# A fused two-block kernel: TensorE products of the identity placed in front of its waits

## The chip, the cores and the metric

The kernel runs on one core of one Trainium2 chip, as one launch. The time is the device time of the whole program in microseconds, taken as the median of several runs. One further run was recorded by the hardware profiler; every row below comes from it.

## The reference

The program computes a first transformer block and then a second block of two layers, for 256 tokens of width 1024 in float32.

- First block: a modulation vector from `c`; `h = modulate(rms_norm(x))`; a token mixer with a retention branch (4 heads) and three groups of dilated attention (12 heads), merged by gates and multiplied by `w_o`; `x = x + g1 * mixer`; then an MLP, `x = x + g2 * (relu(h @ w_ff1)**2) @ w_ff2` with 4096 hidden columns; a final RMS norm.
- Each of the two layers of the second block: an input projection of x; multi-head latent attention (8 heads), an mLSTM (4 heads, two directions) and an SSD scan (4 heads, two directions), whose outputs are joined and multiplied by `w_out`; a residual and a layer norm; then a two-level mixture of experts: router products pick one of 4 groups and 2 of its 4 experts per token, tokens are sorted by group, 16 experts of width 256 are applied, and the result is scattered back; a residual and a layer norm.

## The kernel before, in words

The five engines run programs of their own, written out in order by hand, and meet in semaphores. Weights stream from HBM in units of 128x1024 into a ring of 8 raw slots (SyncE issues the DMAs). ScalarE rounds a unit to `w_hi` (L679), GpSimd or VectorE subtracts to get `w_lo` (L622, L1945), into rings of 4 slots, and TensorE multiplies each unit in three products (`mm3`: hi by hi, hi by lo, lo by hi, L1162 to L1164). A slot is handed on when TensorE increments `unit_used`.

Activations reach TensorE as transposed halves. `turn_x` (L1211) transposes four 128x128 tiles of x or h for each of two halves into the two banks of `T`, and for each half waits for `ready` (VectorE has written it) and for the bank of `T` to be read; ScalarE copies the result (`xT_hi`), VectorE subtracts (`xT_lo`, L1951) and increments `t_lo`. `up_normed` starts a stage: `turn_x` for token tile 0, products of that tile with units 0 to 2, `turn_x` for token tile 1, products with unit 3, then the second tile's products with units 0 to 3. It starts the mixer of the first block, the MLP and each layer.

In the first block's MLP, `clear_acc` zeroes the four banks of `AC`, and `ffn_step` then waits for the squared ReLU (`ffn_h`), transposes it (`turn`, L1288) and runs the products of the next hidden tile.

In a layer, a loop over p (0 to 14, with `N_POS2` = 12) runs at each position some products of the projection and some pieces of the attention: `mla_scores`, `mla_turn` (L1622), `mla_values` (L1632, which waits for ScalarE's copy and VectorE's release). The mixers' loop over h (0 to 4, `LH` = 4) has rows, products and then `ssd_values` (L1745, waits for GpSimd, L658) and `lstm_values` (L1737). After the output product comes the router: `turn_x` for token tile 0, four of its eight router chunks, `turn_x` for tile 1, the other chunks (L1805 to L1808, products with 40 and 20 columns). The routing then waits for VectorE twice: for the chosen group before the ranks (L1823 to L1828), and for the one-hot slots before `gather` (L1835). The experts follow.

PSUM has 8 banks: `T` two, `G` two, `AC` four. TensorE's order is fixed: what stands behind a wait waits too.

Of the kernel before, what the change touches and what calls it, by code (L numbers as in the profile page):

```python
# [25 lines left out]
P = 128  # L26
S = 256
TOK = S // P
# [16 lines left out]
LH, LDH = 4, 64  # L45
# [28 lines left out]
U_MLP = U_WO + 8  # L74
# [4 lines left out]
N_ADA = len(ADA_ORDER)  # L79
# [6 lines left out]
L_IN = 0  # L86
# [4 lines left out]
N_POS2 = 3 * UP  # L91
# [26 lines left out]
LT_X = 0  # L118
# [74 lines left out]
def program(nc, A):  # L193

    ctx = ExitStack()
    with ctx:
# [962 lines left out]
        def _(pe):  # L1159
# [41 lines left out]
                if t == TOK - 1:  # L1201
                    i.then_inc(unit_used, 1)

            def turn_x(n, t, src, ready, at):

                for b in range(2):
                    pe.wait_ge(ready, at + b + 1)
                    if not (isinstance(n, int) and n + b < 2):
                        pe.wait_ge(t_lo, n + b - 1)
                    for c in range(4):  # L1210
                        i = pe.transpose(T[:, b, c * P:(c + 1) * P], src[:, t, b * NT + c * P:b * NT + (c + 1) * P], ident[:, :])  # L1211
                    i.then_inc(t_ready, 1)

            def up_normed(n, k, banks, tn, src, ready, at, turned=None):


                def half(t, u):

                    if u % (UP // HALVES) == 0:
                        pe.wait_ge(t_lo, tn + 2 * t + u // (UP // HALVES) + 1)  # L1220

                turn_x(tn, 0, src, ready, at)
                if turned:
                    turned()
                for u in range(UP):
                    if u == UP - 1:
                        turn_x(tn + 2, 1, src, ready, at + HALVES)
                    half(0, u)
                    up_tile(n, k, u, 0, banks)
                for u in range(UP):  # L1230
                    half(1, u)
                    up_tile(n, k, u, 1, banks)
# [79 lines left out]
            def clear_acc():  # L1312
                for b in range(4):
                    pe.matmul(AC[:, b, :], zero_r[0:1, :], xT_hi[0:1, 0:2, :].rearrange("p c n -> p (c n)"),
                              start=True, stop=False)
# [200 lines left out]
            down_pairs(0, U_WO, T_MERGE, lambda q: tile(10 + q // 2)[:, :, q % 2 * 256:(q % 2 + 1) * 256], 4, merged_head)  # L1516

            mod_sums(5)
            up_normed(0, U_MLP, G, T_H2, h_sb, h_ready, HALVES * TOK, lambda: pe.wait_ge(mod_out, N_ADA))
            pe.wait_ge(zero_ready, 1)  # L1520
            clear_acc()
            with pe.Fori(0, FF_TILES - 2) as e:
                ffn_step(e * 8 + U_MLP, UP, e * 2 + T_MLP, e, tile(1), 4)
            e = FF_TILES - 2
# [15 lines left out]
            for l in range(LAYERS):  # L1540
                n = l * L_UNITS + U_LAYERS
                tb = l * LT + T_LAYERS
                m = l * LM + (M_LAYERS + G_CREDIT)
                up_normed(n, L_IN, G, tb + LT_X, x_sb, x_ready, HALVES * l * TOK)
                for u in range(UP):
                    if u == UP - 1:
                        pe.wait_ge(cq_ready, l + 1)
# [88 lines left out]
                def mlstm_rows(h):  # L1636

                    for j in (2 * h, 2 * h + 1):
                        if j >= 2:
                            pe.wait_ge(lexp_ready, l * 8 + (j - 1))  # L1640
                        row(AC[:, j % 2, :], j % 2 * LH + h, (mask_f, mask_b)[j % 2]).then_inc(lrow_ready, 1)
# [31 lines left out]
                for p in range(N_POS2 + 3):  # L1673
                    if p == 0:
                        pe.wait_ge(kv_out, l * TOK + TOK)
                    if p == UP:
                        pe.wait_ge(q_out, l + 1)
                    if p == 2 * UP:
                        pe.wait_ge(g_free, m + 3)
                    if p < N_POS2 - 2:  # L1680
                        up_unit(n, L_REST + p // UP * UP, p % UP, (G, AC, G)[p // UP])
                    elif p < N_POS2 + 2:
                        half = p - (N_POS2 - 2)
                        up_tile(n, L_REST + N_POS2 - UP, UP - 2 + half // TOK, half % TOK, G)
                    if p in (1, 2):
                        mla_qk_turn(2 * p - 2)
                        mla_qk_turn(2 * p - 1)
                    if p == 3:
                        for k in range(4, 8):
                            mla_qk_turn(k)  # L1690
                    if p == 4:
                        pe.wait_ge(q_out, l + 1)
                        running_sums()
                        conv_turn(0)
                        conv_turn(1)
                    if p == 5:
                        conv_turn(2)
                        pe.wait_ge(sx_out, l * 3 + 2)
                        pe.wait_ge(rows_w, l + 1)
                        for t in range(TOK):  # L1700
                            i = pe.transpose(T[:, 1, t * P:(t + 1) * P], rows_p[:, t, :], ident[:, :])
                        i.then_inc(rows_T, 1)
                    if 4 <= p < 4 + MH:
                        mla_scores(p - 4)
                    if 6 <= p < 6 + MH:
                        if p == 6:
                            pe.wait_ge(sx_out, l * 3 + 3)
                            pe.wait_ge(rows_out, l + 1)
                        mla_turn(p - 6)
                    if p == N_POS2 + 2:  # L1710
                        pe.wait_ge(row_ready, l + 1)
                        pe.wait_ge(lqk_out, l * TOK + TOK)
                        mlstm_rows(0)
                    if 7 <= p < 7 + MH:
                        mla_values(p - 7)
                    if p == N_POS2 + 2:
                        ssd_inputs()
                    if p == 8:
                        pe.wait_ge(g_free, m + 4)
                        for t in range(TOK):  # L1720
                            for c in range(4):
                                a = IN2["mq"] + c * P
                                i = pe.transpose(AC[:, t, c * P:(c + 1) * P], P2[:, t, a:a + P], ident[:, :])
                            i.then_inc(lqk_T, 1)
# [41 lines left out]
                for h in range(LH + 1):  # L1766
                    if h < LH:
                        if h == 0:
                            pe.wait_ge(me_ready, l * MH + MH)
                        for j in (2 * h, 2 * h + 1):  # L1770
                            if j >= 2:
                                pe.wait_ge(sexp_ready, l * 8 + (j - 1))
                            elif j == 1:
                                pe.wait_ge(scb_out, l * SG + 1)
                            row((AC[:, 2, :], T[:, 1, :])[j % 2], 8 + j % 2 * SH + h, (mask_f, mask_b)[j % 2]).then_inc(srow_ready, 1)
                        if h == 0:
                            lstm_products(0)
                        if h + 1 < LH:
                            lstm_products(h + 1)
                            mlstm_rows(h + 1)  # L1780
                    if h >= 1:
                        ssd_values(h - 1)
                        lstm_values(h - 1)
# [7 lines left out]
                nr = EGROUPS + EXPERTS  # L1791

                turn_x(tb + LT_X2, 0, x_sb, x2_ready, HALVES * l * TOK)
                pe.wait_ge(lo_ready, n + (L_ROUTER + 1))
                s = L_ROUTER % SLOTS

# [2 lines left out]
                def router(t, chunks):  # L1799

                    both = AC[:, t, 0:2 * nr].rearrange("p (x n) -> p x n", x=2)
                    for c in chunks:
                        rows = slice(t * P, (t + 1) * P)
                        if c < KC - 1:
                            pe.matmul(both, xT_hi[:, c, rows], w_both[:, :, c, :], start=c == 0, stop=False)  # L1805
                        pe.matmul(both[:, 0, :], xT_lo[:, c, rows], w_both[:, 0, c, :], start=False, stop=False)
                        if c == KC - 1:
                            i = pe.matmul(both, xT_hi[:, c, rows], w_both[:, :, c, :], start=False, stop=True)  # L1808
                            return i

                pe.wait_ge(t_lo, tb + (LT_X2 + 1))
                router(0, range(KC // 2))
                pe.wait_ge(t_lo, tb + (LT_X2 + 2))
                turn_x(tb + (LT_X2 + 2), 1, x_sb, x2_ready, HALVES * (l * TOK + 1))
                router(0, range(KC // 2, KC))
# [2 lines left out]
                pe.wait_ge(t_lo, tb + (LT_X2 + 4))  # L1818
                router(1, range(KC // 2, KC)).then_inc(unit_used, 1)

                pe.wait_ge(route_in, l * 4 + 1)
                rank = AC[:, 2, 0:12].rearrange("p (k n) -> p k n", n=4)
                pe.matmul(rank[:, 2, :], ones, r_g[:, 0, :], start=True, stop=False)  # L1823
# [6 lines left out]
                def gather(q):  # L1830
# [5 lines left out]
                                              start=t == 0 and x is xk_hi, stop=t == 1 and x is xk_lo)  # L1836
                    i.then_inc(t_ready, 1)

                pe.wait_ge(route_in, l * 4 + 3)
                for q in range(UP):  # L1840
                    gather(q)
# [1159 lines left out]
```

## Time and profile before

| | us |
|---|---|
| median of 3 runs | 1404.49 |
| lowest, highest | 1401.08, 1404.7 |
| profiled run, its own time | 1406.39 |
| profiled run, span of the core | 1404.3 |
| TensorE busy (share of the span) | 1309.3 (93%) |
| VectorE busy | 857.3 (61%) |
| ScalarE busy | 735.1 (52%) |
| GpSimd busy | 635.4 (45%) |

The span runs from the first to the last instruction on the core. Times in rows are microseconds from the span's start. TensorE's clock is granted by the chip at one of two levels; a stretch's figure is the mean share of 2.4 GHz, so 0.50 is 1.2 GHz throughout, and a figure between 0.50 and 1.00 is part of each.

### The profile page before, as it was taken

What the parts mean: (1) busy time and instruction counts of PE and PEld (TensorE: products, weight loads), DVE (VectorE), ACT (ScalarE), POOL (GpSimd) and SP (SyncE); (2) the same over time, 40 slices, a digit from 0 to 9 for tenths busy, and PEclk for the clock granted to TensorE, in tenths of its full rate; (3) what the DMA queues carried; (4) which work ended last, traced back from release to release, by engine and by line L of the source; (5) the groups of instructions that cost most, each with busy time, mean ns of one, the idle gap of its engine ahead of it and who ended that gap; (6) DMA issues with size and microseconds to landing.
All of it is one profiled execution on the core that took longest, in us unless ns stands there. A gap on an engine that the chain in (4) does not pass through costs nothing.

```text
span 1404.3 us, 17484 instructions
## 1 busy us (share of the span) xinstructions
PE 1309.3 (93%) x6096; PEld 1066.3 (76%) x6096; DVE 857.3 (61%) x1349; ACT 735.1 (52%) x1090; POOL 635.4 (45%) x516
## 2 busy tenths in 40 slices
PE   6899999999998899999998979999989997799996
PEld 3687777888886688887787767888868786788884
DVE  7574873354344543113677667877867857677778
ACT  4343444454564444445566416666745653467664
POOL 2899889987768689997400410000060024000000
PEclk9999999999999999999999879999999989799998
DMA  9966468635444455454531007878744300577782
GB/s 380 365 237 239 152 237 307 240 150 240 181 154 160 163 180 183 176 200 159 210 121 61 0 15 304 306 291 327 289 190 151 120 1 0 222 294 282 287 308 90
DMA packets 44477, 279.86 MB, mean 199 GB/s; under 512 B 5453, under 2 KB 8781, under 8 KB 12014
## 3 DMA queue, kind: packets, MB, share of 16 engines
q1 hardware_dynamic: 37426, 263.82, 50.6%
q10 hardware_dynamic: 6974, 15.05, 2.9%
q8 instruction: 44, 0.72, 0.2%
q14 instruction: 33, 0.27, 0.1%
HBM read 274.66 MB, written 4.19 MB: 199 GB/s over the span
## 4 chain that ended last, share of the span: by engine, by line
PE 74%; DVE 10%; POOL 8%; DVEq 3%; ACT 2%; issue 2%; DMA 1%; ACTq 0%; SPq 0%; POOLq 0%
PE G L1162 12%; PE G L1164 11%; PE G L1163 11%; PE AC L1162 9%; PE AC L1164 9%; PE AC L1163 9%; POOL w_lo L622 8%; DMA w_raw<-w_stream 1%; DVE w_lo L1945 1%; PE T L1288 1%; DVE arena L2542 1%; ACT w_hi L679 1%; PE G L1737 1%; PE G L1745 1%; DVE sm L1981 1%
## 5 line engine op out<-in xcount | busy, mean ns | idle before, releaser
L622 POOL TENSOR_TENSOR w_lo<-w_raw,w_hi 128x512 fp32r<-128x512 f32 (+1 forms) x474 | 607.3, 1314 | 360.6 <-ACT w_hi L679 352.7
L679 ACT ACTIVATE w_hi<-w_raw 128x1024 fp32r<-128x1024 f32 x448 | 470.8, 1056 | 404.6 <-PE G L1164 192.4
L1945 DVE TENSOR_TENSOR w_lo<-w_raw,w_hi 128x1024 fp32r<-128x1024 f32 x230 | 278.4, 1223 | 65.0 <-ACT w_hi L679 57.3
L1162 PE MATMUL AC<-w_hi,yT_hi 128*128 128x512 f32 x464 | 183.6, 396 | 0.9 <-POOL w_lo L622 0.9
L1162 PE MATMUL G<-w_hi,xT_hi 128*128 128x512 f32 x432 | 178.3, 413 | 3.7 <-DVE xT_lo L1951 1.9
L1163 PE MATMUL AC<-w_lo,yT_hi 128*128 128x512 f32 x464 | 180.9, 390 | 0.0
L1164 PE MATMUL AC<-w_hi,yT_lo 128*128 128x512 f32 x464 | 180.8, 390 | 0.0
L1164 PE MATMUL G<-w_hi,xT_lo 128*128 128x512 f32 x432 | 172.5, 399 | 0.0
L1163 PE MATMUL G<-w_lo,xT_hi 128*128 128x512 f32 x432 | 171.9, 398 | 0.0
L1162 PE MATMUL G<-w_hi,arena_r 128*128 128x512 f32 x320 | 128.0, 400 | 4.7 <-DVE arena L2792 3.4
L1164 PE MATMUL G<-w_hi,arena_r 128*128 128x512 f32 x320 | 125.1, 391 | 0.0
L1163 PE MATMUL G<-w_lo,arena_r 128*128 128x512 f32 x320 | 124.7, 390 | 0.0
L1162 PE MATMUL AC<-w_hi,xT_hi 128*128 128x512 f32 x272 | 110.9, 408 | 4.3 <-POOL w_lo L622 4.2
L1164 PE MATMUL AC<-w_hi,xT_lo 128*128 128x512 f32 x272 | 106.3, 391 | 0.0
L1163 PE MATMUL AC<-w_lo,xT_hi 128*128 128x512 f32 x272 | 106.2, 390 | 0.0
L1162 PEld LDWEIGHTS AC<-w_hi,yT_hi 128*128 128x128 f32 x464 | 87.9, 189 | 20.7 <-POOL w_lo L622 2.1
L1164 PEld LDWEIGHTS AC<-w_hi,yT_lo 128*128 128x128 f32 x464 | 87.8, 189 | 18.5
L1163 PEld LDWEIGHTS AC<-w_lo,yT_hi 128*128 128x128 f32 x464 | 87.9, 189 | 17.5
L1162 PEld LDWEIGHTS G<-w_hi,xT_hi 128*128 128x128 f32 x432 | 83.7, 194 | 21.4 <-DVE xT_lo L1951 2.7
L1164 PEld LDWEIGHTS G<-w_hi,xT_lo 128*128 128x128 f32 x432 | 83.2, 193 | 18.3
L1163 PEld LDWEIGHTS G<-w_lo,xT_hi 128*128 128x128 f32 x432 | 83.9, 194 | 16.4 <-issue 0.2
L2032 DVE SCALAR_TENSOR_TENSOR mod<-w_raw,sm,mod 128x1024 f32<-128x1024 f32 x46 | 82.6, 1795 | 18.3 <-DMA rel_scratch<-arena 8.7
(448 smaller groups left out, 1789.6 us busy)
## 6 DMA issues: line engine op xcount, KB each, us to landing
w_raw<-w_stream SPq DMA_DIRECT2D x152, 1024.0 KB, 4.9
w_raw<-w_expert SPq DMA_DIRECT2D x96, 1024.0 KB, 4.9
mod<-rows ACTq DMA_DIRECT2D x2, 2048.0 KB, 9.2
rel_scratch<-arena ACTq DMA_DIRECT2D x1, 3072.0 KB, 20.6
mod<-rows ACTq DMA_DIRECT2D x3, 476.0 KB, 5.6
x_sb<-x SPq DMA_DIRECT2D x1, 1024.0 KB, 9.2
arena<-const SPq DMA_DIRECT2D x1, 1024.0 KB, 8.3
mod<-gn_g ACTq DMA_DIRECT2D x1, 1024.0 KB, 12.6
```

Of the source, the lines that this page charges most:

```text
L622: i = pool.tensor_tensor(w_lo[:, k % SLOTS, cols], w_raw[:, raw, cols], w_hi[:, k % SLOTS, cols].bitcast(F32), ALU.subtract)
L679: act.activation(w_hi[:, k % SLOTS, cols], w_raw[:, raw, cols], ACT.Copy).then_inc(hi_ready, 1)
L1162: pe.matmul(out, xh, wh, start=start, stop=False)
L1163: pe.matmul(out, xh, wl, start=False, stop=False)
L1164: return pe.matmul(out, xl, wh, start=False, stop=stop)
L1288: i = pe.transpose(T[:, t, c * P:(c + 1) * P], src[:, t, c * P:(c + 1) * P], ident[:, :])
L1737: i = pe.matmul(G[:, 0, c:c + LDH + 1], lw[:, (2 * h + d) % 4, st, t * P:(t + 1) * P], vaug[:, st, h, 0:LDH + 1], start=st == sts[0], stop ...
L1745: i = pe.matmul(G[:, 1, t * S + h * SP_:t * S + (h + 1) * SP_], sw[:, (2 * h + d) % 4, st, t * P:(t + 1) * P], xdt[:, st, d, h * SP_:(h + ...
L1945: dve.tensor_tensor(w_lo[:, k % SLOTS, :], w_raw[:, k % RAW, :], w_hi[:, k % SLOTS, :].bitcast(F32), ALU.subtract).then_inc(lo_ready, 1)
L1981: dve.bn_stats(bst[:, 2 * t + c, :], x_sb[:, t, half(c)])
L2032: dve.scalar_tensor_tensor(m, w_raw[:, raw, :], csil[:, s:s + 1], m, ALU.mult, ALU.add).then_inc(ada_used, 1)
L2542: i = dve.scalar_tensor_tensor(xc[:, c, :], xpad[:, c, k:k + S], cv_w[:, c, k:k + 1], xc[:, c, :], ALU.mult, ALU.add)
```

## The change

A helper `keep_busy(out, count)` issues `count` products of the 128x128 float32 identity with itself into the first 128 columns of a bank. Nothing reads them; a later product that starts its sum afresh overwrites them. It is called in front of waits: 2 and 3 times at the halves of the MLP's first `turn_x`; 7 after `clear_acc`; 7 and 0 at the first layer's first `turn_x`, 10 and 0 at the second's; 5 in the first layer behind the `turn_x` of token tile 1; in both layers 5 at p = `N_POS2`, 4 at h = `LH`, 10 behind the router's first `turn_x`, 2 after its first four chunks, 5 before the ranks and 9 before the gather. That is 34 outside the part that both layers share, and 35 in each layer.

In `turn_x` the wait for the bank of `T` now stands ahead of the wait for the data, with the products between. Two waits are added so that the bank is free: for `lqk_out` at p = `N_POS2`, and for the seventh `sexp_ready` at h = `LH`.

```diff
+            def keep_busy(out, count):
+
+                for k in range(count):
+                    pe.matmul(out[:, 0:P], ident[:, :], ident[:, :], start=True, stop=True)
+
-            def turn_x(n, t, src, ready, at):
+            def turn_x(n, t, src, ready, at, busy=(0, 0)):
 
                 for b in range(2):
-                    pe.wait_ge(ready, at + b + 1)
                     if not (isinstance(n, int) and n + b < 2):
                         pe.wait_ge(t_lo, n + b - 1)
+                    keep_busy(T[:, b, :], busy[b])
+                    pe.wait_ge(ready, at + b + 1)
...
-            def up_normed(n, k, banks, tn, src, ready, at, turned=None):
+            def up_normed(n, k, banks, tn, src, ready, at, turned=None, busy=(0, 0), late=0):
...
-                turn_x(tn, 0, src, ready, at)
+                turn_x(tn, 0, src, ready, at, busy)
...
                         turn_x(tn + 2, 1, src, ready, at + HALVES)
+                        keep_busy(AC[:, 0, :], late)
...
-            up_normed(0, U_MLP, G, T_H2, h_sb, h_ready, HALVES * TOK, lambda: pe.wait_ge(mod_out, N_ADA))
+            up_normed(0, U_MLP, G, T_H2, h_sb, h_ready, HALVES * TOK, lambda: pe.wait_ge(mod_out, N_ADA), (2, 3))
             pe.wait_ge(zero_ready, 1)
             clear_acc()
+            keep_busy(T[:, 0, :], 7)
...
-                up_normed(n, L_IN, G, tb + LT_X, x_sb, x_ready, HALVES * l * TOK)
+                up_normed(n, L_IN, G, tb + LT_X, x_sb, x_ready, HALVES * l * TOK, None, ((7, 0), (10, 0))[l], (5, 0)[l])
...
+                    if p == N_POS2:
+                        pe.wait_ge(lqk_out, l * TOK + TOK)
+                        keep_busy(AC[:, 0, :], 5)
...
+                    if h == LH:
+                        pe.wait_ge(sexp_ready, l * 8 + 2 * LH - 1)
+                        keep_busy(AC[:, 2, :], 4)
...
                 turn_x(tb + LT_X2, 0, x_sb, x2_ready, HALVES * l * TOK)
+                keep_busy(G[:, 1, :], 10)
...
                 router(0, range(KC // 2))
+                keep_busy(G[:, 1, :], 2)
...
+                keep_busy(G[:, 1, :], 5)
                 pe.wait_ge(route_in, l * 4 + 1)
...
+                keep_busy(G[:, 1, :], 9)
                 pe.wait_ge(route_in, l * 4 + 3)
```

## Rows read from the trace of the kernel before

**Rows 1.** The page's chain that ended last, by engine; the core's mean granted clock.
```profile
PE 74%; DVE 10%; POOL 8%; DVEq 3%; ACT 2%; issue 2%; DMA 1%; ACTq 0%; SPq 0%; POOLq 0%
...
core 0: 1404.3 us, clock 0.964
```

**Rows 2.** Stretches: length, busy time of PE, PEld, DVE, ACT, POOL, then PEclk.
```profile
670.90:674.30 3.40, 3.40 (x10) 2.66 (x9) 0.00 (x0) 0.00 (x0) 0.00 (x0) 0.50 1.00 419
...
759.60:797.20 37.60, 35.33 (x200) 29.99 (x199) 20.11 (x56) 22.82 (x55) 10.33 (x16) 0.82 0.00 1
...
824.50:845.00 20.50, 14.70 (x67) 14.46 (x68) 14.37 (x58) 3.68 (x5) 0.00 (x0) 0.50 0.20 75
...
1029.30:1036.10 6.80, 6.25 (x17) 4.62 (x15) 5.93 (x12) 2.06 (x4) 6.80 (x10) 0.50 0.43 158
...
1186.30:1189.70 3.40, 2.11 (x14) 1.62 (x12) 3.26 (x6) 1.09 (x2) 0.23 (x1) 1.00 0.00 0
```

**Rows 3.** TensorE in time order (start, length): 128x512 products, then 128x128 float32 products.
```profile
671.63 0.63 PE L1162 MATMUL G<-w_hi,xT_hi 128*128 128x512 f32 x1
672.06 0.63 PE L1163 MATMUL G<-w_lo,xT_hi 128*128 128x512 f32 x1
...
676.54 0.39 PE L1163 MATMUL G<-w_lo,xT_hi 128*128 128x512 f32 x1
676.77 0.39 PE L1164 MATMUL G<-w_hi,xT_lo 128*128 128x512 f32 x1
...
299.98 0.38 PE L1472 MATMUL AC<-arena 128*128 128x128 f32 x2
300.20 0.39 PE L1473 MATMUL AC<-arena 128*128 128x128 f32 x2
```

**Rows 4.** TensorE in time order at the MLP's and the layers' heads.
```profile
475.52 1.03 PE L1211 MATMUL T<-ident,arena 128*128 128x128 f32 x8
...
486.85 1.97 PE L1288 MATMUL T<-ident,arena 128*128 128x128 f32 x8 [2.35 <-DVE arena L2309]
...
661.36 1.27 PE L1211 MATMUL T<-ident,x_sb 128*128 128x128 f32 x8 [2.31 <-issue]
...
670.50 0.50 PE L1162 MATMUL G<-w_hi,xT_hi 128*128 128x512 f32 x1 [1.85 <-POOL w_lo L622]
...
1028.33 1.52 PE L1211 MATMUL T<-ident,x_sb 128*128 128x128 f32 x8 [3.35 <-DVE x_sb L2362]
```

**Rows 5.** VectorE in time order: what the second token tile waits for.
```profile
475.13 0.69 DVE L2022 TENSOR_TENSOR arena<-AC,mod 128x512 f32<-128x512 f32 x1
...
1035.99 1.41 DVE L2362 SCALAR_TENSOR_TENSOR x_sb<-AC,sm,mod 128x512 f32<-128x512 f32 x2
```

**Rows 6.** TensorE in time order, the first layer's mixers.
```profile
758.08 1.08 PE L1632 MATMUL AC<-mod,arena 128*128 128x64 f32 x8 [2.00 <-DVE arena L2535]
...
782.05 1.55 PE L1745 MATMUL G<-arena 128*128 128x64 f32 x12
783.44 1.50 PE L1737 MATMUL G<-arena 128*128 128x65 f32 x12
786.47 2.42 PE L1745 MATMUL G<-arena 128*128 128x64 f32 x12 [1.52 <-POOL arena L658]
788.68 2.77 PE L1737 MATMUL G<-arena 128*128 128x65 f32 x12
```

**Rows 7.** ScalarE in time order: the last attention copy in each layer.
```profile
762.19 0.60 ACT L964 ACTIVATE arena<-T 128x512 f32<-128x512 f32 x1 [0.83 <-PE T L1622]
...
1128.62 0.60 ACT L964 ACTIVATE arena<-T 128x512 f32<-128x512 f32 x1 [1.30 <-PE T L1622]
```

**Rows 8.** Waits of TensorE at the router: total, times, longest.
```profile
PE AC L1805 <- DVE xT_lo L1951: 6.4, 2, 3.2
```

**Rows 9.** TensorE in time order, the first layer's routing.
```profile
836.19 0.59 PE L1823 MATMUL AC<-sm,arena 128*128 128x4 f32 x2 [1.77 <-DVE sm L2417]
...
841.33 5.68 PE L1835 MATMUL AC<-xT_lo,arena_r 128*128 128x256 f32 x32 [2.85 <-DVE xT_lo L2740]
```

## The prediction

> **What bounds the kernel.** I read the page's chain first [rows 1]: TensorE holds 74% of it, VectorE 10%, GpSimd 8%. So a microsecond taken from TensorE's own work counts, unless another engine's wait stands behind it. The granted clock came next: a mean of 0.964, where 0.50 is 1.2 GHz and 1.00 is 2.4 GHz, so (1 - 0.964) x 2 x 1404.3 = 101 us of the span ran at 1.2 GHz. Then stretches around each dip [rows 2]. They lie where the products are put: behind the first layer's head (670.9 to 674.3), in the mixers (0.82 over 37.6 us, so 13.5 us at 1.2 GHz), from the router to the gather (20.5 us), at the second layer's head (6.8 us); the second layer repeats mixers and router. The MLP has two such places (at its head and behind `clear_acc`). Last came TensorE in order of time, for what the engine did before a fall: at the places shown it had stood in a wait of 1.5 to 3.4 us [rows 4, 6, 8].
>
> What a fall costs is in two pairs of rows [rows 3]: products of 128x512 start 0.43 us apart at 1.2 GHz (672.06 - 671.63) and 0.23 us apart at 2.4 GHz (676.77 - 676.54), so 0.20 us a product. Eight transposes take 1.97 us against 1.03 [rows 4].
>
> **The price of an added product.** The nearest rows are float32 products of 128x128 [rows 3]: two records each, and the next starts 0.22 us later at 2.4 GHz. At 1.2 GHz no row has this form; with the ratio of the rows above it is 0.43 us, and the trace gives no reason for less than 0.22 or more than 0.44. At 0.22 us: 7 are 1.5 us before the wait of 2.31 ends at the first layer's head, 5 are 1.1 us in 1.85 (late) and in 2.00 (p = 12), 4 are 0.9 us in 1.52 (h = 4), 10 are 2.2 us in 3.35 at the second layer's head [rows 4, 6]; 7 are 1.5 us in 2.35 behind `clear_acc`. All of them end before the data comes, so at full clock they cost nothing. The swapped order in `turn_x` costs nothing either: both waits must end anyway, and `T` is free first at these places. The two added waits: `lqk_out` is counted up by ScalarE at its p = 10, before the copies that TensorE needs at p = 12; the seventh `sexp_ready` must come before GpSimd's last product, which is what `ssd_values` waits for anyway [rows 6]. Behind both stand only instructions that already wait longer. Cost 0; if `lqk_out` were late, the units of p = 13 and VectorE's copies behind them would be.
>
> **What each place gives back, if the clock stays at 2.4 GHz there.**
>
> 1. MLP head (2 and 3). The first products run at 1.2 GHz and could gain over 1 us, but the second tile's transposes (475.52) start while VectorE still writes that tile's second half, until 475.13 + 0.69 = 475.82 [rows 4, 5]. TensorE would be early and wait there. Bounds 0 to 0.5, I take 0.1.
> 2. Behind `clear_acc` (7). Transposes 1.97 - 1.03 = 0.9 us, and some 3 products before the clock returns, 0.6 us [rows 3, 4]. Behind it the MLP runs dense, with nothing for TensorE to be early for. I take 1.5.
> 3. First layer's head (7 and 5). 3.4 us at 1.2 GHz with 3.4 us of products [rows 2]: 3.4 / 0.43 = 8 products, 8 x 0.20 = 1.6, less the partial ones at its edges, 1.5 us. They release the first ring slot, on which ScalarE, GpSimd and TensorE's next tile wait in turn, so all of it shifts.
> 4. p = 12 (5). ScalarE waited 0.83 us (first layer) and 1.30 us (second) for TensorE's last attention transposes, and starts the mixers' exponentials behind them [rows 7]. Before these waits ScalarE is the later one, so they are the bound: 0.8 + 1.3 = 2.1 us.
> 5. h = 4 (4). `ssd_values` and `lstm_values` took 2.42 + 2.77 us laid out from 786.47 to 791.24, 4.8 us, where the same two took 2.9 us from 782.05 to 784.94 [rows 6]: 1.9, with the transposes behind them 2.1 us in each layer. VectorE's normalisation of the heads, which the output product waits for later, starts from them, so it moves as well. The products between are faster too, but end at VectorE's wait and add nothing. 2 x 2.1 = 4.2 us.
> 6. Second layer's head (10). 6.8 us at 1.2 GHz with 6.25 us of work [rows 2] would be over 2.5 us. But the second tile is written by VectorE until 1035.99 + 1.41 = 1037.40 [rows 5], and it is only its first transposes (1.52 against 1.03 for eight [rows 4]) that bring VectorE forward. Bounds 0.2 to 1.0, I take 0.4.
> 7. Router and routing (10, 2, 5, 9 in each layer). Here I don't expect the clock to be held. In the 20.5 us TensorE was busy for 14.7 us and still got 0.50 throughout [rows 2]: its work there is products with 40, 20 or 4 columns, and two added products in the middle change little. The 10 (2.2 us in the longest wait, 3.2 [rows 8]) should put the fall off by some 2 to 3 us, which makes part of the second tile's transposes and a few router products faster: about 0.5 us. Then the 5 and the 9 start at 1.2 GHz: 5 x 0.43 = 2.2 us in a wait of 1.77, 0.4 late; 9 x 0.43 = 3.9 us in 2.85, 1.0 late [rows 9]. Against this, 9 added products and the gather form one dense run, so the clock should return some 2 us earlier than in the 5.68 us of the gather, about 0.7 to 1.0 us. Sum between -1.4 (late, nothing back) and +3 us (all at full clock) a layer; I take 0, since gain and loss are of one size.
>
> Sum: 0.1 + 1.5 + 1.5 + 2.1 + 4.2 + 0.4 + 0 = 9.8 us. The profiled run took 1406.39 us (span 1404.3 and 2.1 around it); 1406.39 - 9.8 = 1396.6. It lies 1.9 us above the median of 1404.49, inside their spread of 3.6, so the same sum from the median is 1394.7. **I predict 1395 us.**
>
> **A rule weighed.** In rows 2, at 1186.3 to 1189.7, TensorE was busy for 2.11 of 3.40 us, of which eight transposes are 1.03 [rows 4], and the clock stayed at 1.00. The Trainium skill (TensorE: Matmul & The Clock Gate, Part 4: PE-mode transpose) says that a transpose doesn't count as a busy array in the way a product does. By it that stretch would have been nearly empty and the heads, where transposes are half of what stands in the gaps, would fall in spite of the added products. By the row they count.
>
> **Rivals.**
>
> A. Other engines take the gain. VectorE's chains in steps 4 and 5 may have been only just behind TensorE, as at steps 1 and 6. For it: those two steps show the pattern. Against it: the 0.83, 1.30 us of waiting for TensorE [rows 7]. It would leave steps 2, 3 and 6 and lose 1 us at the router: 3.4 - 1 = 2.4, 1402.
>
> B. The added products do not hold the clock at all (an identity is mostly zeros, or the engine wants more than that). Then everything stays but the late ends of step 7, 2 x 1.4 = 2.8: 1404.5 to 1407.3, I say 1406. Against it: no row shows that data matters; none excludes it.
>
> C. Slower: products that are too long for their gap at 1.2 GHz. The mechanism is that of step 7, and it decides the sum if the clock is already at 1.2 GHz when the gap opens, elsewhere too: 10 in 3.35 is 0.95 late, 7 in 2.31 0.7, 5 in 1.85 0.3, 4 in 1.52 twice 0.2, 5 in 2.00 twice 0.15 [rows 4, 6], and 2.8 at the router: 5.5 us, with nothing back, 1410. Against it: at those gaps the clock was still full before; only in the last two of the router was it not [rows 2, 9].
>
> D. Transposes don't count. Steps 1, 3 and 6 go, since they hang on the heads: 9.8 - 2.0 = 7.8, 1396.7. By the row above this is unlikely.
>
> E. The router is held too. Then both layers gain up to 3 us more: 1389. For it, that 26 products are put there; against it, the 14.7 us of narrow products at 0.50.
>
> Also open within the forecast: where the falls land depends on where a run happens to stand, so that a place may fall in one run and not in the next. At h = 4 the added products end 0.6 us before narrow ones (64 and 65 columns), so it is the place likeliest to fall anyway, for 2 us.
>
> **Numbers.** Forecast 0.60 (1391 to 1399 by the bounds of its steps and one place missed), A 0.15, B 0.09, C 0.06, D 0.04, E 0.06. A measurement of this kernel tells about 0.3%, 4.2 us, from no change. Faster by more takes the forecast, D, E and a fourth of A: 0.60 + 0.04 + 0.06 + 0.04 = 0.74. Within 0.3%: the rest of A, B, and C's mild end: 0.11 + 0.09 + 0.01 = 0.21. Slower: 0.05. The range, 1390 to 1402, leaves out B, C and E's low end.
>
> **What would show it.** The mean clock should rise from 0.964 to about 0.98, with half-clock stretches left mainly between router and gather, in both layers. Step 2: transposes at L1288 near 486 back at 1.03 us. Step 3: no wait of the first layer's products changed, the products behind it 0.23 us apart. Step 4: ScalarE's waits at L964 gone, its own copy before them last. Step 5: the last L1745 group at about 1.5 us instead of 2.4. Steps 1 and 6: a new wait of TensorE for VectorE ahead of the second tile's transposes, 1 to 2 us. Step 7: the group before the ranks ending behind `route_in`, and the gather starting later after the ranks than the 2.85 us of before, but taking less than 5.68. The forecast is wrong if the clock stays low behind the added products (B), if the router holds 1.00 (E), or if mixers run faster and the output product starts no earlier (A).

## The result, and the profile after

The changed kernel takes 1394.39 us (median of 4 runs, 1394.00 to 1394.94) against 1403.65 us for the kernel before (4 runs, 1401.08 to 1404.70): a ratio of 0.9935, interval 0.9915 to 0.9954. The interval is a 95% one. A ratio is estimated from all runs of both kernels, and differs by up to 0.1% (1.5 us) from the quotient of the two medians, so that below a gain is often given both ways. The forecast was 1395.0 in a range of 1390 to 1402. The profiled run took 1394.94 us, 11.45 less than the profiled run of before, which at 1406.39 us lay above all four runs given here. One run of all that follow, in experiment 1, took 1507.59 us at a mean clock of 0.829; it is left out of the ratios.

The page of the changed kernel: TensorE's busy time, the granted clock in 40 slices of the span (9 is 90% of full speed or more), and the chain by engine.

```profile
PE 1318.5 (95%) x6304; PEld 1076.9 (77%) x6304; DVE 856.6 (61%) x1349; ACT 733.9 (53%) x1090; POOL 634.4 (46%) x516
...
PEclk9999999999999999999999979999999999899998
...
PE 74%; DVE 12%; POOL 7%; DVEq 3%; ACT 2%; issue 1%; DMA 1%; ACTq 0%; POOLq 0%
```

TensorE still holds 74% of the chain [rows 1]; VectorE rose from 10% to 12%. The lowest slices are now those of the router (twice) and of the end. The same stretches as in rows 2, moved to where that work now lies and, for the mixers, 3 us shorter (length, busy time of PE, PEld, DVE, ACT, POOL, then PEclk):

```profile
669.20:672.60 3.40, 3.40 (x16) 2.77 (x15) 0.00 (x0) 0.56 (x1) 0.00 (x0) 1.00 1.04 434
756.40:791.00 34.60, 32.47 (x216) 27.49 (x215) 20.20 (x57) 22.47 (x55) 10.35 (x16) 1.00 0.00 1
818.50:839.00 20.50, 19.26 (x98) 19.10 (x99) 14.04 (x57) 3.68 (x5) 0.00 (x0) 0.58 0.21 80
1023.40:1030.20 6.80, 5.04 (x22) 3.38 (x20) 5.93 (x12) 2.07 (x4) 6.80 (x10) 1.00 0.48 158
```

Layer head, mixers and second layer head are at 1.00, where they were at 0.50, 0.82 and 0.50. The router is at 0.58 against 0.50, though TensorE is busy for 19.26 of 20.5 us instead of 14.70. Over the run, the time at 1.2 GHz fell from 102 us to 50, and the mean clock rose from 0.964 to 0.982.

Where the 11.3 us between the two spans come from is read by following the same instruction through both traces. The shift is its start after less its start before:

| TensorE instruction | before | after | shift | gained since the mark above |
|---|---|---|---|---|
| MLP: transposes behind `clear_acc` | 486.85 | 486.76 | -0.09 | 0 (step 1; the run already stood at -0.14 ahead of the MLP) |
| first layer's head | 661.36 | 659.70 | -1.66 | 1.57 (step 2) |
| p = 12's transposes | 755.48 | 752.29 | -3.19 | 1.53 (step 3) |
| `mlstm_rows(0)` | 763.29 | 759.25 | -4.04 | 0.85 (step 4) |
| transposes of the output product's third pair | 801.48 | 795.11 | -6.37 | 2.33 (step 5) |
| first expert product | 848.00 | 842.07 | -5.93 | -0.44 (step 7) |
| second layer's head | 1028.33 | 1022.43 | -5.90 | 0 |
| its second tile | 1037.29 | 1031.02 | -6.27 | 0.37 (step 6) |
| p = 12's products | 1124.04 | 1118.00 | -6.04 | -0.23 |
| `mlstm_rows(0)` | 1129.72 | 1122.37 | -7.35 | 1.31 (step 4) |
| third pair | 1168.32 | 1158.22 | -10.10 | 2.75 (step 5) |
| first expert product | 1215.21 | 1204.00 | -11.21 | 1.11 (step 7) |

TensorE in time order at the heads; L1207 is the added product (two records each), and the bracket is the idle time before a group and what ended it.

```profile
475.84 0.63 PE L1217 MATMUL T<-ident,arena 128*128 128x128 f32 x4 [0.81 <-DVE arena L2040]
484.37 1.83 PE L1207 MATMUL T<-ident 128*128 128x128 f32 x14
486.76 1.09 PE L1295 MATMUL T<-ident,arena 128*128 128x128 f32 x8 [0.56 <-DVE arena L2327]
657.27 1.72 PE L1207 MATMUL T<-ident 128*128 128x128 f32 x14
659.70 1.38 PE L1217 MATMUL T<-ident,x_sb 128*128 128x128 f32 x8 [0.70 <-DVE x_sb L2392]
1018.91 2.39 PE L1207 MATMUL T<-ident 128*128 128x128 f32 x20
1022.43 1.38 PE L1217 MATMUL T<-ident,x_sb 128*128 128x128 f32 x8 [1.12 <-DVE x_sb L2380]
1031.02 1.29 PE L1217 MATMUL T<-ident,x_sb 128*128 128x128 f32 x8 [1.66 <-DVE x_sb L2380]
```

Each group of added products ends before the data comes: 0.56, 0.70 and 1.12 us of waiting are left. Behind `clear_acc` the transposes are back to 1.09 us from 1.97 [rows 4]. At 475.84 and 1031.02 stand the two new waits for VectorE (0.81 and 1.66), where TensorE is now early.

The first layer's mixers, with ScalarE's last attention copy in front:

```profile
758.08 0.58 ACT L964 ACTIVATE arena<-T 128x512 f32<-128x512 f32 x1
```

```profile
752.73 1.28 PE L1207 MATMUL AC<-ident 128*128 128x128 f32 x10
754.89 1.08 PE L1640 MATMUL AC<-mod,arena 128*128 128x64 f32 x8 [0.89 <-DVE arena L2553]
...
780.75 1.11 PE L1207 MATMUL AC<-ident 128*128 128x128 f32 x8
782.43 1.55 PE L1756 MATMUL G<-arena 128*128 128x64 f32 x12 [0.58 <-POOL arena L658]
783.82 1.50 PE L1748 MATMUL G<-arena 128*128 128x65 f32 x12
...
795.11 0.66 PE L1295 MATMUL T<-ident,arena 128*128 128x128 f32 x4 [2.33 <-DVE arena L2678]
```

The kernel before, the transposes behind its last values, and the wait at the third pair:

```profile
791.24 1.06 PE L1288 MATMUL T<-ident,arena 128*128 128x128 f32 x4
...
801.48 0.66 PE L1288 MATMUL T<-ident,arena 128*128 128x128 f32 x4 [0.48 <-DVE arena L2660]
```

ScalarE's copy, which waited 0.83 us for TensorE [rows 7], has no wait left: ScalarE itself is now the later one. The last values take 2.73 us laid out (782.43 to 785.16) instead of 4.77 (786.47 to 791.24, where the transposes below start). The output product behind them also runs at full clock and then stands 2.33 us for VectorE (0.48 before), so what it gains is given back as waiting. VectorE's chain that ends this wait takes the same time in both traces; it only starts 6.37 us earlier (before, then after):

```profile
793.10 0.16 DVE L2624 SCALAR_TENSOR_TENSOR sm<-arena 128x8 f32<-128x8 f32 x1
...
800.35 1.07 DVE L2660 TENSOR_TENSOR arena<-arena 128x512 f32<-128x512 f32 x1
```

```profile
786.73 0.16 DVE L2642 SCALAR_TENSOR_TENSOR sm<-arena 128x8 f32<-128x8 f32 x1
...
793.99 1.06 DVE L2678 TENSOR_TENSOR arena<-arena 128x512 f32<-128x512 f32 x1
```

The router and routing of the first layer:

```profile
815.04 2.40 PE L1207 MATMUL G<-ident 128*128 128x128 f32 x20
...
821.21 1.94 PE L1217 MATMUL T<-ident,x_sb 128*128 128x128 f32 x8 [1.24 <-DVE x_sb L2380]
...
827.93 2.48 PE L1207 MATMUL G<-ident 128*128 128x128 f32 x10
830.20 0.43 PE L1840 MATMUL AC<-sm,arena 128*128 128x4 f32 x2
...
832.20 4.19 PE L1207 MATMUL G<-ident 128*128 128x128 f32 x18
836.03 5.06 PE L1852 MATMUL AC<-xT_lo,arena_r 128*128 128x256 f32 x32
842.07 0.50 PE L1162 MATMUL G<-w_hi,arena_r 128*128 128x512 f32 x1 [0.98 <-DVE w_lo L1963]
```

The clock has fallen by 821.21 (eight transposes in 1.94 us). From there the added products are too long for their gaps: from ranks to gather it is 836.03 - 830.20 = 5.83 us, 5.14 before [rows 9], so 0.69 late, and the gather gives 0.62 back (5.06 for 5.68).

How much of this is a matter of the single run is seen in all traces together. The time from the router's first transposes to the first expert product, in us:

| kernel | first layer | second layer | both |
|---|---|---|---|
| no router products: before | 27.46 | 27.83 | 55.29 |
| experiment 1 | 27.53 | 27.71 | 55.24 |
| experiment 2 | 27.52 | 27.89 | 55.41 |
| experiment 10 | 27.54 | 27.63 | 55.17 |
| experiment 11 | 27.54 | 27.84 | 55.38 |
| 10 and 2 only: experiment 6 | 27.32 | 27.87 | 55.19 |
| 10, 2, 5, 9: the change | 27.91 | 26.73 | 54.64 |
| experiment 3 | 27.37 | 27.89 | 55.26 |
| experiment 4 (transposes) | 26.86 | 27.78 | 54.64 |
| experiment 12 | 25.87 | 27.59 | 53.46 |
| 10, 6, 3, 6: experiment 7 | 24.99 | 25.39 | 50.38 |
| products between the chunks: experiment 8 | 25.59 | 25.93 | 51.52 |
| experiment 9 | 24.63 | 26.03 | 50.66 |

Without router products the sum hardly moves (55.2 to 55.4). With the change's four counts it is 53.5 to 55.3, on average 0.8 us shorter, and which layer gains differs from trace to trace.

### The profile page after: what moved, and what is told of

Read it like the earlier page. It is cut to its first block, busy times and chain, and to the rows that moved or that the text cites. A ratio compares the mean times of both kernels' runs of the same rounds, so it can differ in the third digit from the quotient of the medians.

```text
span 1393.0 us, 17897 instructions
## 1 busy us (share of the span) xinstructions
PE 1318.5 (95%) x6304; PEld 1076.9 (77%) x6304; DVE 856.6 (61%) x1349; ACT 733.9 (53%) x1090; POOL 634.4 (46%) x516
## 4 chain that ended last, share of the span: by engine, by line
PE 74%; DVE 12%; POOL 7%; DVEq 3%; ACT 2%; issue 1%; DMA 1%; ACTq 0%; POOLq 0%
PE G L1162 11%; PE G L1164 11%; PE G L1163 11%; PE AC L1162 9%; PE AC L1164 9%; PE AC L1163 9%; POOL w_lo L622 7%; DVE w_lo L1963 1%; DVE mod L2050 1%; PE T L1295 1%; PE G L1207 1%; DVE arena L2560 1%; DVE sm L1999 1%; ACT w_hi L679 1%; DMA w_raw<-w_stream 1%
## 5 line engine op out<-in xcount | busy, mean ns | idle before, releaser
L1162 PE MATMUL G<-w_hi,xT_hi 128*128 128x512 f32 x432 | 175.3, 406 | 3.2 <-DVE xT_lo L1969 1.9
L1164 PE MATMUL G<-w_hi,xT_lo 128*128 128x512 f32 x432 | 169.3, 392 | 0.0
L1163 PE MATMUL G<-w_lo,xT_hi 128*128 128x512 f32 x432 | 169.0, 391 | 0.0
```

Source lines behind the costliest of these rows:

```text
L1162: pe.matmul(out, xh, wh, start=start, stop=False)
L1163: pe.matmul(out, xh, wl, start=False, stop=False)
L1164: return pe.matmul(out, xl, wh, start=False, stop=stop)
```

## The experiments

Each ran beside the kernel before on the same chip. Experiments 1 to 4 share its runs of 1403.54 us (median of 19, 1400.90 to 1406.97), 5 to 8 those of 1404.54 (17 runs), 9 to 12 those of 1405.62 (17 runs). The change itself was measured apart from them, so a difference between an experiment and the change is one between two sets of runs, perhaps on two chips.

**1. The waits and the order without the products.**

```diff
-                for k in range(count):
+                for k in range(0):
```

> Every call of keep_busy issues 0 products; the swapped order in turn_x and the two added waits stay. Theory (the added products hold the clock, nothing else in the change acts): the time of before, 1403 +- 2, mean clock back to 0.96 to 0.97, half-clock stretches back in the MLP, at both layer heads, at p = 12 and in the mixers. Rival (the order of the waits moves the time): 1395 to 1399 with the clock as low as before.

Measured: 1406.50 us (10 runs, 1403.01 to 1409.86 and one of 1507.59; 1406.40 without that one), ratio 1.0014 [0.9997, 1.0031], mean clock 0.967. That is 3 us above before by the medians and 2 by the ratio, whose interval takes in no change; the 1401 to 1405 us expected was missed by 1.5. The swapped order in `turn_x` and the two added waits bring nothing (they may cost up to 4 us by the interval); the gain is the products'.

**2. All products but the router's, and 3. the router's alone.** In the first the four counts 10, 2, 5, 9 are 0; in the second all others are.

```diff
-                keep_busy(G[:, 1, :], 10)
+                keep_busy(G[:, 1, :], 0)
... (likewise 2, 5 and 9)
```

> The router's and routing's products (10, 2, 5, 9 in each layer) are 0, all others stay. Theory (step 7 gives about nothing): 1393 to 1396, like the changed kernel, within 1.5 us of it. Rival (the router's products carry part of the gain): 1397 or more. Second rival (they cost, being late at 1.2 GHz): 1392 or less. In the trace the ranks should follow the router's last product by 1.77 us and the gather the ranks by 2.85, as before.

> Only the router's and routing's products stay (52 in all); the others are 0. Theory: within 2 us of the kernel before, 1402 to 1405. Rival (router carries part of the gain): 1400 or less.

Measured: 1396.15 us (4 runs, 1395.83 to 1396.17), ratio 0.9937 [0.9913, 0.9962], and 1402.35 us (10 runs), 0.9987 [0.9973, 1.0001]. So the router's products bring 1.8 us by the medians of 2 and of the change, 1.3 by their spans (1394.3 and 1393.0), and 1.2 by themselves. The prediction had 0. By the ratios, 0.9937 for experiment 2 and 0.9935 for the change, they bring almost nothing, so their share is small and not measured well; between the two traces, 0.8 us of the 1.3 lie in the router stretches. Experiment 2 came out between its expectation (at most 1396) and its rival (from 1397); experiment 3 as expected.

**4. Transposes in place of products.** Two transposes of the identity take nearly the time of one float32 product (14 in 1.75 us behind `clear_acc`, against 1.83 for 7 products).

```diff
-                for k in range(count):
-                    pe.matmul(out[:, 0:P], ident[:, :], ident[:, :], start=True, stop=True)
+                for k in range(2 * count):
+                    pe.transpose(out[:, 0:P], ident[:, :], ident[:, :])
```

> Each added product is replaced by two transposes of the identity, of the same length together (0.11 us each at full clock). Theory (transposes count for the clock like products): 1394 to 1396, clock 0.98. Rival D (a transpose doesn't count): falls come back at the heads and mixers, 1402 to 1405, clock 0.965.

Measured: 1394.86 us (4 runs, 1393.95 to 1395.05), ratio 0.9927 [0.9902, 0.9951], clock 0.983: the same as the change. The two stretches of head and mixers in it:

```profile
669.20:672.60 3.40, 3.40 (x17) 2.79 (x16) 0.00 (x0) 0.66 (x1) 0.00 (x0) 1.00 0.96 400
756.40:791.00 34.60, 32.38 (x217) 27.34 (x216) 20.20 (x57) 22.41 (x55) 10.36 (x16) 1.00 0.00 1
```

**5. Narrow products.** As many products at the same places with as many weight loads, 16 columns wide.

```diff
-                    pe.matmul(out[:, 0:P], ident[:, :], ident[:, :], start=True, stop=True)
+                    pe.matmul(out[:, 0:16], ident[:, :], ident[:, 0:16], start=True, stop=True)
```

> Each added product keeps its 128x128 weights but has 16 columns instead of 128, so TensorE issues the same number of instructions and loads the same weights while its array streams an eighth of the columns. Theory (the clock follows the columns that stream, as the router's narrow products at 0.50 suggest): the gain is gone, 1401 to 1405, clock 0.965 to 0.97. Rival (any issued product or weight load counts): 1394 to 1396, clock 0.98.

Measured: 1403.87 us (10 runs), ratio 0.9995 [0.9984, 1.0006], clock 0.966, and 95 us at 1.2 GHz in the trace (102 before, 50 in the change): the whole gain is gone, as expected. At h = 4 the eight records last nearly as long as the wide ones (1.02 against 1.11 us), the wait behind them is as long (0.66 against 0.58), and still the clock falls:

```profile
784.50 1.02 PE L1207 MATMUL AC<-ident 128*128 128x16 f32 x8
786.18 1.55 PE L1756 MATMUL G<-arena 128*128 128x64 f32 x12 [0.66 <-POOL arena L658]
787.57 2.26 PE L1748 MATMUL G<-arena 128*128 128x65 f32 x12
789.62 1.06 PE L1295 MATMUL T<-ident,arena 128*128 128x128 f32 x4
```

So what held the clock here was not that TensorE issued something, nor that the profile calls it busy.

**6. The router without its late products.** 10 and 2 stay, 5 and 9 are 0.

> At the router 10 and 2 stay, the 5 before the ranks and the 9 before the gather are 0; all else as in the changed kernel. Without any router products the time was 1396.15, with all 1394.39. Theory 1 (the early ones put off the fall, the late ones pay for themselves at best): 1394.5 to 1395.5. Rival (the late ones, which join with the gather into a dense run, bring the 1.8 us): 1396 or more. In the trace the ranks follow the last router product by 1.8 us and the gather the ranks by 2.85.

Measured: 1395.78 us (4 runs, 1395.36 to 1396.50), ratio 0.9938 [0.9921, 0.9955]. Experiment 2 lies 0.4 us above it (spans 1394.3 and 1393.7), the change 1.4 below (1393.0, so 0.7 by the spans). That falls between the two expectations (up to 1395.5, from 1396), and the three ratios (0.9937, 0.9938, 0.9935) don't separate the kernels. By medians and spans the late products carry the larger part, in spite of starting at half clock and ending late. In the traces they cost 0.6 us in the first layer (27.32 to 27.91), where the clock returns at 838.4 us here and at 838.3 in the change, and give 1.1 in the second (27.87 to 26.73). There one sees how; first this experiment's gather, then the change's:

```profile
1197.90 6.62 PE L1852 MATMUL AC<-xT_lo,arena_r 128*128 128x256 f32 x32 [2.85 <-DVE xT_lo L2758]
```

```profile
1194.21 4.19 PE L1207 MATMUL G<-ident 128*128 128x128 f32 x18
1198.05 4.96 PE L1852 MATMUL AC<-xT_lo,arena_r 128*128 128x256 f32 x32
```

The nine products and the gather form one dense run, and the clock is back in the middle of the gather, at 1200.1 us (1203.7 in experiment 6).

**7. The counts fitted to the gaps.** 10, 6, 3 and 6.

```diff
-                keep_busy(G[:, 1, :], 2)
+                keep_busy(G[:, 1, :], 6)
...
-                keep_busy(G[:, 1, :], 5)
+                keep_busy(G[:, 1, :], 3)
...
-                keep_busy(G[:, 1, :], 9)
+                keep_busy(G[:, 1, :], 6)
```

> At the router 10, 6, 3, 6 instead of 10, 2, 5, 9: more where the wait is long and at full clock, fewer where 5 x 0.43 and 9 x 0.43 us run past their waits. Theory (the lateness of 0.3 and 1.0 us a layer is on the path): ranks and gather start when their data comes, 1393 to 1394. Rival (the later return of the clock takes back what the earlier start gives): 1394 to 1395, no different from the changed kernel.

Measured: 1392.64 us (5 runs, 1391.13 to 1393.23), ratio 0.9912 [0.9897, 0.9926]: below both expectations, and all of its runs below all of the change's.

```profile
820.22 1.58 PE L1207 MATMUL G<-ident 128*128 128x128 f32 x12
822.15 1.28 PE L1217 MATMUL T<-ident,x_sb 128*128 128x128 f32 x8 [0.35 <-DVE x_sb L2380]
826.45 1.63 PE L1207 MATMUL G<-ident 128*128 128x128 f32 x6
829.05 0.59 PE L1840 MATMUL AC<-sm,arena 128*128 128x4 f32 x2 [0.98 <-DVE sm L2435]
831.21 2.91 PE L1207 MATMUL G<-ident 128*128 128x128 f32 x12
834.20 4.76 PE L1852 MATMUL AC<-xT_lo,arena_r 128*128 128x256 f32 x32
```

Six instead of two in front of the second tile leave 0.35 us of its wait (1.24 in the change), and the fall comes later: the tile's transposes are at full clock, half clock lasts 10.2 us in each layer instead of 17.1 and 13.6. From the router's first transposes to the first expert product it is 24.99 us, 27.91 in the change and 27.46 in the kernel before. Over both layers the stretches are 4.3 us shorter than in the change, the whole time only 1.8: in this trace the clock also fell for 3.4 us at the second layer's head (from 1030.3), where it held in the change with the same products.

**8. One product behind each chunk of the router**, so that the narrow products hardly stand alone. The helper stands behind the `return` of a token tile's last chunk, so it is 14 a layer (60 records more than in the change, 4 of them from the 3 in place of 2).

```diff
+                        keep_busy(G[:, 1, :], 1)
...
-                keep_busy(G[:, 1, :], 2)
+                keep_busy(G[:, 1, :], 3)
```

> One added product behind each chunk of the router (14 in a layer) besides 10, 3, 5, 9. They lengthen the router's own run by 0.22 us each at full clock, 2.6 us behind the second transposes, but should hold the clock through router, ranks and gather. Theory (the router can be held, and what is saved, 24 narrow products at 0.11 instead of 0.21, transposes 0.9, ranks 1.0 and the lateness of 5 and 9, is more than the price): half-clock stretch between router and gather gone, 1390 to 1393. Rival (clock still falls, products at 0.43 on the path): 1397 to 1402.

**9. One behind every second chunk.** `c % 2` picks chunks 1, 3, 5 and 7, and 7 is the last one, which returns first: 6 a layer, not the 8 (and 16) of which the expectation speaks. The trace has 40 records more than the change's: 2 x 6 products between the chunks and 2 x 4 from the 6 in place of 2.

```diff
+                        keep_busy(G[:, 1, :], c % 2)
...
-                keep_busy(G[:, 1, :], 2)
+                keep_busy(G[:, 1, :], 6)
```

> Between the router's chunks a single identity product stands only behind every second chunk (8 a layer instead of 16), with 10, 6, 5 and 9 at the four places. With one behind each chunk no half-clock stretch was left between router and gather, at a cost of 16 x 0.22 = 3.5 us a layer. Theory (the clock is held with half of them): about 1.8 us a layer less to pay, 1389 to 1390.5 us, mean clock 0.99. Rival (half of them is too thin and the clock falls in the router): 1392.5 to 1394 us, a stretch of about 10 us at half clock in each layer.

Measured: 1392.77 us (6 runs, 1391.87 to 1394.88), ratio 0.9918 [0.9904, 0.9932], clock 0.993; and 1391.19 us (5 runs, 1390.32 to 1393.43), ratio 0.9908 [0.9891, 0.9926], clock 0.989. The router's stretch, first in experiment 8, then in 9:

```profile
818.50:839.00 20.50, 17.46 (x144) 16.51 (x144) 15.48 (x59) 6.12 (x9) 0.00 (x0) 1.00 0.27 105
```

```profile
818.50:839.00 20.50, 16.34 (x134) 15.45 (x134) 16.37 (x61) 7.28 (x11) 0.00 (x0) 1.00 0.34 133
```

The router can be held at full clock; then the gather takes 4.1 us and what stands behind it is VectorE:

```profile
832.58 4.08 PE L1853 MATMUL AC<-xT_lo,arena_r 128*128 128x256 f32 x32 [1.35 <-DVE xT_lo L2759]
838.49 0.50 PE L1162 MATMUL G<-w_hi,arena_r 128*128 128x512 f32 x1 [1.84 <-DVE w_lo L1964]
```

From the router's first transposes to here it is 24.63 us in experiment 9 and 25.59 in 8, so in the first layer fewer than half of the products hold it too, and cheaper. But in 9 the clock fell again in the second layer (0.72 over 1187 to 1203), so both of its theories are half right: held in one layer, not in the other, and the median lies between their ranges. Experiment 8 came out as expected. The median of 9 is the lowest of all, 3.2 us under the change; 7, 8 and 9 lie within 1.6 us of each other with overlapping intervals, and their order isn't settled.

**10. Only the mixers' products (5 and 4), and 11. only those of the MLP and the layers' heads**, all other counts 0. What the expectations call marks are the rows of the table of shifts above.

> Only the 5 at p = 12 and the 4 at h = 4 are kept, with their two waits; all other places 0. Theory (the sum is made of separate places): by the marks of the two traces 0.85 + 1.31 at p = 12 and 2.33 + 2.74 at h = 4 = 7.2 us under before, 1396 to 1397.5 us; by the prediction's terms 6.3, 1397 to 1398.5. Rival (the mixers' places need the heads' clock, or other places fall in their stead): above 1400 us.

> Only the MLP's places (2, 3, 7) and those of the two layer heads (7, 5 late, 10) are kept; mixers and router 0. Theory: by the marks 0 + 1.57 + 1.53 + 0.37 = 3.5 us under before, 1400 to 1401.5 us, as the prediction's terms have it too (3.5). Rival (these heads release ring slots on which others wait, so the mixers behind them lose or gain as well): more than 1.5 us away from that on either side.

Measured: 1399.19 us (5 runs, 1398.30 to 1399.74), ratio 0.9960 [0.9945, 0.9975]; and 1401.55 us (11 runs, 1400.38 to 1404.31), ratio 0.9978 [0.9965, 0.9990]. Against their shared before of 1405.62 these are 6.4 and 4.1 us (by the ratios of all runs 5.6 and 3.1). The times expected were missed, by 0.7 us at least in 10 and by 0.05 in 11; before lay 2.0 us higher here than for the change, which may be why, but isn't shown. With experiment 3's 1.8 the three parts add up to 10.5 us by the ratios, for 9.1 of the whole (interval 6.5 to 11.9): within these intervals no part needs another.

**12. The change without the 4 at h = 4** (their wait stays).

```diff
-                        keep_busy(AC[:, 2, :], 4)
+                        keep_busy(AC[:, 2, :], 0)
```

> The changed kernel without the 4 products at h = 4 (their wait stays). Theory (products in front of that wait alone hold the clock for the last values of the mixers): the clock falls there again in both layers, the groups of L1756 and L1748 go back from 1.5 us to about 2.4 to 2.8, and by the marks 2.33 + 2.74 = 5.1 us come back: 1399 to 1400 us; by the prediction's term 4.2: 1398.6. Rival (the 5 at p = 12 carry the clock across h = 4 too, since they stand before it): within 1.5 us of the change, 1394.5 to 1396 us.

Measured: 1399.43 us (7 runs, 1397.86 to 1400.76), ratio 0.9965 [0.9952, 0.9977]: 5.0 us above the change by the medians, 4.2 by the ratios, as expected. The first layer, and the stretch of its fall:

```profile
782.57 1.95 PE L1756 MATMUL G<-arena 128*128 128x64 f32 x12 [1.62 <-POOL arena L658]
784.32 2.77 PE L1748 MATMUL G<-arena 128*128 128x65 f32 x12
```

```profile
783.60:790.20 6.60, 6.09 (x27) 5.38 (x27) 3.87 (x12) 2.97 (x5) 0.00 (x0) 0.50 0.00 0
```

With 1.62 us of wait and no products in it, the clock falls where it held with four of them. The group of L1748 is back at 2.77 us. This is the largest single place: about half of the gain.

## Why the prediction was right, step by step

The mechanism was right: the products hold the clock (without them, experiment 1, nothing is gained), outside the router they end before the data, and the gain is what ran at 1.2 GHz behind each wait, up to the next wait for another engine. The full-clock price is 0.22 us (20 records in 2.40, less the overlap of the last), the half-clock price 0.43 (18 in 832.20 to 836.03: 3.83 for nine), both as estimated.

- **Step 1** (0.1): 0 measured. TensorE became early and waits 0.81 us for VectorE [rows 5], as said.
- **Steps 2 and 3** (1.5 and 1.5): 1.57 and 1.53.
- **Step 4** (2.1): 0.85 + 1.31 = 2.16. ScalarE's waits [rows 7] were indeed the bound.
- **Step 5** (4.2): 2.33 + 2.75 = 5.1 in the traces, 4.2 to 5.0 by taking it out (experiment 12). The path was as said: VectorE's chain starts earlier and the output product's own gain ends at its wait. The size was taken too low. In the first layer the values gain 2.04 us and not 1.9 (the prediction laid the slow pair out to the next start, 4.8, and the fast one to its last record's end, 2.9; alike they are 4.77 and 2.73), and the transposes with ScalarE's and VectorE's copies behind them 0.3. In the second layer of the kernel before, both groups of values ran at half clock from the start (5.18 us laid out), so there the values gain 2.45; the prediction had read the first layer only.
- **Step 6** (0.4): 0.37, and the new wait of 1.66.
- **Step 7** (0, bounds -1.4 to +3 a layer): -0.44 and +1.11 in the traces, 1.3 to 1.8 for both by experiment 2 (almost nothing by its ratio). The router isn't held, as said; the ends are late, though less than worked out (0.33 and 0 us at the ranks of the two layers for 0.4, 0.69 and 0.85 at the gather for 1.0); and the early products put the fall off by 3.0 and 3.4 us of the work's own time (821.20 + 6.3 against 824.50, 1186.44 + 10.1 against 1193.14), worth 0.4 to 0.6 by experiments 2 and 6. What the late ones give back was set equal to their cost. By experiment 6 it is larger by 0.6 to 1.4 us over both layers, all of it in the second (gather 1.66 us shorter), and the stretches in the other traces with these counts show that the second layer's gain is one of this run. A fair size for the step is 0.8 us over both layers, from 0 to 1.8 by trace.

The sum of 9.8 met 9.3 by the medians and 11.3 by the two spans: steps 5 and 7 were 0.9 and 0.7 us too low against the traces. That the forecast of 1395 came within 0.6 us of the median is partly luck, since the medians of the kernel before range from 1403.5 to 1405.6 us in the four sets of runs. The difference between 9.3 and 11.3 lies mostly in the kernel before: the time at half clock in it varies from run to run. The trace of experiment 1, which issues the same products as before, has 93 us of it where the trace of before has 102, 6.8 for 13.7 of them in the second layer's mixers, and a span 3.0 us shorter.

**The rivals.** A (others take the gain) holds only in part: the new or longer waits for VectorE at steps 1, 5 and 6 (0.81, 2.33 and 1.66 us) take what is beyond the measured gains. B (an identity doesn't hold the clock) is refuted by the change itself: an identity, mostly zeros, holds it, as long as it is streamed 128 columns wide and not 16 (experiment 5). Whether full data would do more isn't tested. C needs a clock that is low when the gap opens; of the places that were given products, only the router's late ones had that. D (transposes don't count) is refuted by experiment 4: transposes alone, in the same gaps, gave 1394.86 and 0.983. The Trainium skill (TensorE: Matmul & The Clock Gate, Part 4: PE-mode transpose) says that the transpose mode doesn't count as a busy array in the same way; here the measurement decides against it. E (the router held too, 1389) didn't happen with these counts; experiments 8 and 9 show that it can be made to, but for 6 to 14 products in each layer between the chunks, and with VectorE's waits behind them, so that 1391 to 1393 us is reached and not 1389.

What stays open: why the same counts hold the router in one layer and not in the other (experiment 9), and how much the router's products of the change bring (0.3 us by the ratios, 1.3 by the spans, 1.8 by the medians) and how it divides between the early and the late ones.

## What to carry to other kernels

Where TensorE, at full clock, waits 1.5 to 3.4 us for another engine, products into a free bank in front of the wait can hold the clock: here 0.65% for 104 float32 products of 128x128, about half of it from the 8 at h = 4. Between narrow products, as in the router, it takes more of them and isn't certain. Size them to end just before the data at the price of the clock that stands there (0.22 us each at 2.4 GHz, 0.43 at 1.2); don't save on their width (16 columns held nothing where 128 did); and put them first where the work behind the wait is what other engines wait for. Look behind each place for the engine that is late next, since it caps the gain (at the output product the wait grew from 0.48 to 2.33 us).

## What the runs showed of the hardware beyond the forecast

- The clock fell behind a wait of 1.62 us between groups of products 64 and 65 columns wide (experiment 12). Once in the changed kernel it fell behind a wait that the change itself had lengthened, 2.31 us at 1158.22, though in the first layer it held behind 2.33 us at the same place:

```profile
1158.22 0.66 PE L1295 MATMUL T<-ident,arena 128*128 128x128 f32 x4 [2.31 <-DVE arena L2678]
```

```profile
1159.20:1162.50 3.30, 3.30 (x9) 2.64 (x8) 3.01 (x4) 0.03 (x1) 3.30 (x5) 0.50 0.00 0
```

- In the change's first router TensorE's records are busy for 19.26 of 20.5 us at a granted clock of 0.58: a busy engine wasn't a fast one there.
- Runs of the kernel before spread over 8 us (1400.9 to 1408.9 in 53 runs), those of the change over 0.9 and of experiment 2 over 0.3 (4 runs each). It isn't simply that fewer falls mean less spread: experiments 8 and 9, with clocks of 0.987 to 0.993, spread over 3.0 and 3.1 us.
